# The first b block of a fused decoder layer: seven products in place of four plain quarters, with the operand slots renamed

## What is computed

```python
    z = jnp.einsum("btd,dc->btc", xn, w_in)
    u, v, b_gate, c_gate, x_in, r_a, r_b = jnp.split(z, SPLITS, axis=-1)
    ...
    y_a = jnp.einsum("btc,cd->btd", u * chunk_spatial_mix(v, w_s, b_s), w_a_out)
    ...
    y_b = jnp.einsum("btc,cd->btd", b_gate * short_conv(xp, conv_w), w_b_out)
    h = jax.nn.sigmoid(r_a) * y_a + jax.nn.sigmoid(r_b) * y_b
    out = jnp.einsum("btd,de->bte", h, w_o)
```

## Time and profile before

| What | Value |
|---|---|
| Time, median of 3 runs | 1595.23 us (1594.76 to 1595.33) |
| Time of the profiled execution | 1594.81 us |
| Its span, first to last instruction | 1593.1 us |
| TensorE matmul busy | 1583.8 us, 12361 matmuls |
| VectorE, ScalarE, GpSimd busy | 999.7, 561.7, 707.8 us |
| DMA | 187.27 MB, mean 118 GB/s |
| Granted TensorE clock | 0.999 |

### The profile page before, as it was taken

One profiled execution on the slowest core, in us unless ns is written; L12 is line 12 of the kernel. 1 busy time (PEld: TensorE's weight loads), 2 busy tenths in 40 slices (PEclk: granted clock), 3 DMA queues, 4 the chain that ended last, 5 costly groups with the idle time before them and its releaser, 6 DMA issues.

```text
span 1593.1 us, 30063 instructions
## 1 busy us (share of the span) xinstructions
PE 1583.8 (99%) x12361; PEld 1535.1 (96%) x12361; DVE 999.7 (63%) x1371; ACT 561.7 (35%) x868; POOL 707.8 (44%) x521
## 2 busy tenths in 40 slices
PE   9999999999999999999999999999999999999998
PEld 6889999999999999999978899999999999999998
DVE  7757856686683337768875574544444456685865
ACT  4223332222223335334333632222222234453544
POOL 1011444545544444535640325444444444565675
PEclk9999999999999999999999999999999999999999
DMA  6202011422413333465333402533343356673723
GB/s 220 76 1 80 28 54 34 127 76 65 126 60 129 107 107 108 153 206 181 120 114 120 146 28 74 160 107 107 107 107 107 107 147 173 214 239 107 240 106 134
DMA packets 155842, 187.27 MB, mean 118 GB/s; under 512 B 7403, under 2 KB 138083, under 8 KB 155451
## 3 DMA queue, kind: packets, MB, share of 16 engines
q1 hardware_dynamic: 152635, 182.41, 36.2%
q10 hardware_dynamic: 3072, 2.95, 0.6%
HBM read 133.74 MB, written 48.72 MB: 115 GB/s over the span
## 4 chain that ended last, share of the span: by engine, by line
PE 97%; DMA 1%; POOL 0%; SPq 0%; ACT 0%; issue 0%; DVE 0%; POOLq 0%; ACTq 0%; DVEq 0%
PE ps L439 92%; PE ps L474 2%; PE ps L551 1%; DMA tp_f<-ht_dram 1%; PE ps L534 0%; PE ps L449 0%; PE ps L733 0%; PE ps L717 0%; SPq L1032 0%; ACT tp L1709 0%; DVE tp L2508 0%; PE ps L528 0%; POOL x_late L1240 0%; DVE g L2610 0%; POOLq L178 0%
## 5 line engine op out<-in xcount | busy, mean ns | idle before, releaser
L439 PE MATMUL ps<-tp,ring_hi 128*128 128x258 f32 x7226 | 1173.5, 283 | 1.0 <-DVE g L2613 0.7
L439 PEld LDWEIGHTS ps<-tp,ring_hi 128*128 128x128 f32 x7226 | 1001.8, 190 | 2.1 <-issue 1.9
L439 PE MATMUL ps<-tp,ring_lo 128*128 128x258 f32 x3624 | 740.4, 283 | 0.0
L439 PEld LDWEIGHTS ps<-tp,ring_lo 128*128 128x128 f32 x3624 | 567.8, 190 | 0.0
L1168 POOL TENSOR_TENSOR ring_lo<-ring_f,ring_hi 128x512 fp32r<-128x512 f32 (+1 forms) x240 | 344.4, 1456 | 343.5 <-DVE ring_f L1986 209.2
L1168 POOL TENSOR_TENSOR ring_lo<-stage,ring_hi 128x512 fp32r<-128x512 f32 (+1 forms) x196 | 289.9, 1488 | 408.8 <-ACT ring_hi L1313 408.5
L1313 ACT ACTIVATE ring_hi<-ring_f 128x512 fp32r<-128x512 f32 (+1 forms) x240 | 149.9, 625 | 505.0 <-DVE ring_f L1981 166.8
L1313 ACT ACTIVATE ring_hi<-stage 128x512 fp32r<-128x512 f32 (+1 forms) x196 | 120.3, 618 | 229.6 <-PE ps L439 160.1
L1978 DVE TENSOR_TENSOR ring_f<-stage 128x512 f32<-128x512 f32 (+1 forms) x60 | 59.4, 990 | 99.0 <-DMA stage<-in_w_in 52.4
L439 PE MATMUL ps<-tp 128*128 128x512 f32 (+1 forms) x384 | 72.0, 340 | 0.0
L439 PEld LDWEIGHTS ps<-tp 128*128 128x128 f32 x384 | 59.0, 189 | 8.1
(11 more groups left out here) (271 smaller groups left out, 1447.6 us busy)
## 6 DMA issues: line engine op xcount, KB each, us to landing
stage<-in_w_in SPq DMA_DIRECT2D x24, 1024.0 KB, 5.9
ht_dram<-ht SPq DMA_DIRECT2D x44, 258.0 KB, 4.5
hid_dram<-hq SPq DMA_DIRECT2D x40, 258.0 KB, 3.0
stage<-in_w_gate SPq DMA_DIRECT2D x10, 1024.0 KB, 7.1
stage<-in_w_up SPq DMA_DIRECT2D x10, 1024.0 KB, 5.4
tp_f<-ht_dram SPq DMA_DIRECT2D x16, 516.0 KB, 6.4
stage<-in_w_down SPq DMA_DIRECT2D x8, 1024.0 KB, 5.3
tp_f<-hid_dram SPq DMA_DIRECT2D x12, 516.0 KB, 8.4
```

The costliest lines, as they stand in the source:

```text
L439: ins = pe.matmul(o, w, xc, start=first and n == 0, stop=last and n == 2, skip_group_check=onto)
```

## The change

Block 28 leaves `QORDER` and takes the seven-product form. Slot 0, free during the last three a blocks, now holds quarter 0 (p0) in place of quarter 1, which is no longer loaded. The operands of p3, p1 and p2 are loaded as block 27 finishes its products 0, 1 and 2, and those of p4, p5 and p6 as it finishes 4, 5 and 6. Splits and rests move to new places in the queues, s1 of the a blocks moves ahead of the last weight parts, and TensorE's order interleaves blocks 27, 28 and 29. `H_SLOT` and `O_SLOT` follow the renamed slots. `B_ORDER` is the order in which the b operands become ready.

```diff
-SLOT_M = [2, 0, 1, 6, 3, 4, 7, 5]
+SLOT_M = [0, 3, 1, 7, 2, 6, 4, 5]
-H_SLOT = [0, 2, 3, 1]
+H_SLOT = [3, 0, 2, 1]
+B_ORDER = [0, 3, 1, 2, 4, 5, 6]
-QORDER.update({b: (1, 3, 0, 2) for b in (B_B, B_F, B_UP0)})
+QORDER.update({b: (1, 3, 0, 2) for b in (B_F, B_UP0)})
-O_SLOT = {1: 4, 3: 7, 5: 6, 7: 5}
+O_SLOT = {1: 6, 3: 4, 5: 7, 7: 5}
 # TensorE
-            for i in range(4):
-                bank_free(B_B - 1, PLAIN_BANK[i])
-                half(B_B, i, PLAIN_BANK[i], lambda q: (b_lo, (3, 1, 4, 2)[q]))
-            for r in range(B_B + 1, B_F):
+            for r in range(B_B, B_F):
                 for p in range(7):
-                    if r == B_B + 1 and p in (1, 3, 4, 6):
-                        pe.wait_ge(b_lo, (1, 3, 4, 6).index(p) + 5)
+                    if r == B_B:
+                        pe.wait_ge(b_lo, B_ORDER.index(p) + 1)
                     product(r, p)
 # SyncE, for b in range(B_A, B_F)
                 if b == B_A + 1:
                     sp.wait_ge(prod_done, BASE[B_A + 1])
-                    ob_load(1)
+                    b_load(0)
                 if b + 2 < B_F:
                     load(b + 2)
                 if b == B_B - 1:
-                    for i, n in enumerate((3, 0, 2)):
+                    for p, i in ((3, 0), (1, 1), (2, 2)):
                         sp.wait_ge(prod_done, done(b, i))
-                        ob_load(n)
-                if b + 1 < B_F:
+                        b_load(p)
+                    gate_load_one(b + 1, 0, SPILL[0])
+                    for p, i in ((4, 1), (5, 2), (6, 3)):
+                        sp.wait_ge(prod_done, done(b, p))
+                        b_load(p)
+                        gate_load_one(b + 1, i, SPILL[i])
+                elif b + 1 < B_F:
                     gate_load(b + 1)
 # ScalarE
             for r in range(B_A + 1, B_B):
-                s1(r)
+                if r == B_A + 1:
+                    s1(r)
                 if r < B_B - 1:
                     prepare(r + 1, 0, 5)
                     if r == B_A + 1:
-                        b_split(1)
+                        b_split(0)
+                    s1(r + 1)
                     prepare(r + 1, 5)
                 else:
+                    prepare(r + 1, 0, 2)
                     b_split(3)
-                    prepare(r + 1, 0, 1)
-                    b_split(0)
-                    prepare(r + 1, 1, 2)
+                    prepare(r + 1, 2, 3)
+                    b_split(1)
+                    prepare(r + 1, 3, 5)
                     b_split(2)
-                    prepare(r + 1, 2)
+                    s1(r + 1)
+                    prepare(r + 1, 5, 6)
+                    b_split(4)
+                    prepare(r + 1, 6)
-            bt_split(0)
-            prepare(B_B + 1, 0, 2)
-            bt_split(1)
-            prepare(B_B + 1, 2, 4)
-            bt_split(2)
+            b_split(5)
+            prepare(B_B + 1, 0, 1)
+            b_split(6)
+            prepare(B_B + 1, 1, 6)
             s1(B_B + 1)
-            prepare(B_B + 1, 4, 6)
-            bt_split(3)
             prepare(B_B + 1, 6)
 # VectorE
+            def b_rest(p):
+                dve.wait_ge(b_hi, B_ORDER.index(p) + 1)
+                dve.tensor_tensor(slot(SLOTS_M[p], 1), slot_f(SLOTS_M[p], 1), slot_v(SLOTS_M[p], 0), SUB).then_inc(b_lo, 1)
 # VectorE, a blocks; last is r == 27
                 c22(r, s_turn[(r + 1) % 2][:, :], s_c[:, :])
+                if last:
+                    b_rest(3)
                 sums(r + 1, 2)
                 a_gate(r, 3, s_turn[(r + 1) % 2][:, :], c22_done)
                 c12(r, s_c[:, :])
                 if last:
                     b_rest(1)
                 sums(r + 1, 3)
                 a_gate(r, 1, s_c[:, :], c12_done)
+                dve.wait_ge(a_gated, at_r + 2)
+                c21(r, s_turn[r % 2][:, :])
                 if last:
                     b_rest(2)
-                dve.wait_ge(a_gated, at_r + 2)
-                c21(r, s_turn[r % 2][:, :])
                 a_gate(r, 2, s_turn[r % 2][:, :], c21_done)
                 if r == B_A + 1:
                     b_rest(0)
-                elif last:
-                    b_rest(3)
-            for i, n in enumerate(QORDER[B_B]):
...
-                sums(B_B + 1, i)
-                bt_rest(i)
 # VectorE, b blocks
-            for mp, r in enumerate(range(B_B + 1, B_F), 1):
+            for mp, r in enumerate(range(B_B, B_F)):
+                if mp == 0:
+                    b_rest(4)
                 sums(r + 1, 0)
...
                 b_gate(r, 0, reg(Y, both), s_turn[(r + 1) % 2][:, :], prod_done, done(r, 2))
+                if mp == 0:
+                    b_rest(5)
                 u2(r)
                 u4(r, s_c[:, :])
                 sums(r + 1, 1)
+                if mp == 0:
+                    b_rest(6)
```

More of the change, by code:

```diff
@@ L135, in h_order @@
 def h_order(mp):
-    return QORDER[B_B] if mp == 0 else (0, 3, 1, 2)
+    return 0, 3, 1, 2
 def slots_of(b):
@@ L583, in c11_read @@
                 if b < B_F:
-                    return a_gated, 4 * (b - B_B - 1 + MP - 1) + 1
+                    return a_gated, 4 * (b - B_B + MP - 1) + 1
                 if b < B_D:
@@ L922, in _, with b_load, gate_load_one @@
             bt_save(MP - 1)
[L924 to L931, removed]
+            def b_load(p):
+                if p in D_ROWS:
+                    n, src, count = D_ROWS[p], ob_dram, t_in
+                    sp.wait_ge(q_saved[n], 16 * MP)
+                else:
+                    n, src, count = D_TOTAL[p], bt_dram, total_in
+                    sp.wait_ge(ht_saved[n], 16 * MP)
+                sp.dma_start(slot_f(SLOTS_M[p], 1), src[n]).then_inc(count[n], 16)
+            def gate_load_one(b, i, n):
+                if b == B_A:
+                    sp.wait_ge(q_saved[n], 16 * 3 * MP)
+                elif b - 1 in QORDER:
+                    sp.wait_ge(pl_dve, PL_DVE[b - 1] + i + 1)
+                else:
+                    sp.wait_ge(a_gated, 4 * (b - 2 - B_A) + i + 1)
+                sp.dma_start(q[:, n], (ra_dram, rb_dram)[(b - B_A) // MP][b % MP, :, n]).then_inc(gate_in[n], 16)
             def gate_load(b, parts=None):
                 for i, n in enumerate(parts or (QORDER[b - 1] if b - 1 in QORDER else SPILL)):
[L935 to L943, removed]
+                    gate_load_one(b, i, n)
             for b in range(B_RA, B_A):
@@ L999, in _ @@
             res_load(1)
-            sp.wait_ge(a_gated, 8 * (MP - 1))
+            sp.wait_ge(a_gated, 4 * (2 * MP - 1))
             sp.dma_start(post_gain, mix_post_g[0:1, :].to_broadcast((128, D)).rearrange("p (n c) -> p n c", n=4)).then_inc(post_in, 16)
@@ L1497, in _, with b_split @@
                 gate(2, c21_done, r)
[L1499 to L1505, removed]
+            def b_split(p):
+                act.wait_ge(*((t_in[D_ROWS[p]], 16) if p in D_ROWS else (total_in[D_TOTAL[p]], 16)))
+                act.activation(slot(SLOTS_M[p], 0), slot_f(SLOTS_M[p], 1), ACT.Copy).then_inc(b_hi, 1)
             at_split(3)
@@ L1528, in h_split @@
                 act.wait_ge(h_ready, 4 * mp + i + 1)
-                act.wait_ge(prod_done, done(B_F - 1, mp - 1) if mp else done(B_B, 1))
+                act.wait_ge(prod_done, done(B_F - 1, mp - 1) if mp else done(B_B - 1, 3))
                 act.activation(h_of(n, 0, mp), g[:, 2 * mp + n // 2, n % 2], ACT.Copy).then_inc(h_hi, 1)
@@ L2338, in h_rest @@
                 dve.tensor_tensor(h_of(n, 1, mp), g[:, 2 * mp + n // 2, n % 2], h_of(n, 0, mp).bitcast(f32), SUB).then_inc(h_lo, 1)
-            for i, n in enumerate(QORDER[B_B]):
-                part, tmp = g[:, n // 2, n % 2], (s_b, s_c)[i % 2]
-                dve.wait_ge(prod_done, done(B_B, i))
-                dve.wait_ge(gate_in[n], 16 * (MP + 1))
-                if i >= 2:
-                    dve.wait_ge(h_ready, i - 1)
-                dve.tensor_tensor(tmp, reg(PLAIN_BANK[i], both), q[:, n], MUL).then_inc(pl_dve, 1)
-                dve.wait_ge(pl_dve, PL_DVE[B_B] + i + 1)
-                dve.tensor_tensor(part, part, tmp, ADD).then_inc(h_ready, 1)
-                sums(B_B + 1, i)
-                bt_rest(i)
             def b_gate(r, i, src, gated, ready, count=None):
@@ L2357, in b_gate @@
                 dve.tensor_tensor(gated, src, q[:, n], MUL).then_inc(a_gated, 1)
-                dve.wait_ge(a_gated, 4 * (MP + mp - 2) + i + 1)
+                dve.wait_ge(a_gated, 4 * (MP + mp - 1) + i + 1)
                 dve.tensor_tensor(part, part, gated, ADD).then_inc(h_ready, 1)
-            for mp, r in enumerate(range(B_B + 1, B_F), 1):
+            for mp, r in enumerate(range(B_B, B_F)):
                 last = r == B_F - 1
+                if mp == 0:
+                    b_rest(4)
                 sums(r + 1, 0)
-                dve.wait_ge(h_ready, 4 * mp)
+                if mp:
+                    dve.wait_ge(h_ready, 4 * mp)
                 if last:
```

10 lines of the change are left out of this document (removed).

## The result

The changed kernel takes 1600.58 us (median of 5 runs, 1600.36 to 1602.67) beside 1595.06 for the kernel before on the same chip: ratio 1.0037, 95% interval 1.0023 to 1.0052, 5.5 us slower. The sign and the size were forecast (1599.3 us), but one term was missing from the sum, and so was one wait. The profiled execution took 1601.03 us, its span is 1599.3 us.

The account below looks back on a forecast made before the run. TensorE, busy 99% of the span, was taken as the bound. Waits 2.2 + 1.6 + 3.65 = 7.45 less 3.4 give +4.1 us: 1594.8 + 4.1 = 1598.9, median 0.4 above, 1599.3; range 1595.3 to 1602.4 us.

Parts of the forecast that it names:

- VectorE's chain: VectorE's queue of rests, sums and gates in block 28, ahead of p1, p2 and p5: u2 done at 734.7.
- the disputed term: What GpSimd holds VectorE's operations in block 28: 6 x 1.10 + 2 x 0.37 = 7.3 us; at zero, 1593.1 us.
- Rival (a): VectorE is held less because GpSimd's parts fall into other gaps; at zero waits 1593.5 us; chance 0.26.
- The stands: TensorE in block 28 stands 2.2 us ahead of p1 and 3.65 us ahead of p5, waiting for VectorE.
- The stand ahead of p2: TensorE in block 28 runs p1 until 720.75, then stands 1.6 us until rest p2 is done at 722.35.
- the clock: Rival: the 3.65 us stand ahead of p5 lowers TensorE's clock to 1.2 GHz: 1602 to 1605 us; chance 0.06.
- the forecast 4.1: Whole kernel: TensorE's waits of 2.2 + 1.6 + 3.65 = 7.45 us, less 3.4 us gained: +4.1 us.
- the rest of p6: VectorE's rest p6 and c22 end at about 738.9, p6 due at 740.5: later waits zero.
- Edits at nothing: Renamed slots, moved s1 and the loads of p4, p5 and p6 cost nothing; cover over 5 us for each rest.
- Rival (c): A transfer decides: p5 lands more than 6 us later than worked out; from 1600 us up; chance 0.03.
- The gain of 3.4 us: Block 28: 24 fewer matmuls save 2.89 us, the plain block's holes and excess taken as 0.5; worth 3.4 us without new waits.

## Why the prediction was right, and what it lacked

**VectorE's chain: right.** The rests were forecast to end at 711.5, 717.85, 722.35, 727.3 and, with u2 behind p5's, at 734.7; the rows show 711.60, 717.83, 722.36, 727.39 and 734.73. Of the holds, 7.3 us forecast, the rows show the short ones at 1.79, 1.78, 1.79 and 1.78 against 0.70 (4 x 1.09), two rests at 3.29 and 3.40 against 2.30 (2.1), one rest at 2.79 and an addition at 1.08 with 0.5 and 0.4 more: 7.3 us. The run without the holds gave 1593.38 us where the working gave 1593.1 for holds of zero, and so the disputed term is shown. (Rival (a) names 1593.5 us for the same case; the sum gives 1593.1.)
The lock by the Trainium skill (SBUF — State Buffer, section "SBUF: two separate sides") was worked out as 1.30 for each full wait; in the changed kernel, too, they cost 1.0 to 1.1, so the rows of before were the better price.

**The stands: 2.6 and 3.5 where 2.2 and 3.65 were forecast.** For p1 TensorE was free 0.2 us sooner than the 715.6 taken, and 0.10 us pass from the rest's end (717.83) to the first matmul (717.93); for p5 it was free at 731.4, by the modelled end, and not 731.05.

**The stand ahead of p2: did not come, for a reason the forecast lacked.** Its operand was ready at 722.36, as forecast. But p1, for the most part at half clock, still kept TensorE busy then, and p2 began at 722.41, right behind the rest. The 1.6 us of the sum turned up as 1.6 us of slow p1; the run with filled stands shows the exchange, with 1.4 us ahead of p2.

**A term that was missing: the clock.** The prediction made it a rival of its own, with 0.06, in place of a term of the sum, and its argument was that the rows of before show no long stand. They show none because none was there; nothing in them spoke for a clock that stays. It also looked only at the stand ahead of p5. In fact the clock fell behind both stands. The slow p1 fell into the wait for p2 and cost nothing net; the slow p5 took 1.4 us more than at full clock. With this term the forecast 4.1 becomes 5.5, beside 5.5 (timed) and 6.2 (profiled). The rival's own price, once or twice 2.89 us, was too high: the clock was low for 3.4 us, where a product wholly at the lower level would take 24 x 0.215 = 5.2 us.
The Trainium skill (TensorE: Matmul & The Clock Gate, section "Why this matters for your kernels") says that an idle gap between bursts brings back half rate; here the trace agrees, with 0.64 and 0.67 in the stretches behind the two stands. The gaps that the page warns of are longer than the first of these stands, and the measurement decides: 2.6 us was enough here, and 2.2 us in the kernel with the order alone.

**A wait that was overlooked: the rest of p6.** The prediction let this rest and c22 be due with p6 at 740.5, and put all waits behind p5 at nothing. The rest of p6 is due before p0 of block 29, at 734.7 + 2.89 = 737.6, and by the prediction's own times it ends at 738.2: 0.6 us late. The runs at full clock show that wait (3.46 in place of 2.89 us behind p5 with the stands filled). So at full clock the forecast's sum would have been 4.7 us, and the slow p5 adds 0.9 to that, not 1.4. That the change shows no such wait is the slow p5's doing: two omissions share one place, and the total hides the smaller one.

**Edits at nothing: right, with less cover for one.** The first splits began at 707.33 and 710.34, as before. ScalarE's timeline for p5 and p6, beside the earlier trace rows:

```profile
721.69 1.94 ACT L1503 ACTIVATE tp<-tp_f 128x2064 fp32r<-128x2064 f32 x1 [0.25 <-DMA tp_f<-ob_dram]
...
726.48 1.94 ACT L1503 ACTIVATE tp<-tp_f 128x2064 fp32r<-128x2064 f32 x1 [2.34 <-DMA tp_f<-bt_dram]
```

ScalarE waited for both, so they landed just ahead of 721.7 and 726.5, where 721.3 and 725 were forecast. Their rests began at 730.7 and 736.0: over 7 us of cover each. Rival (c) was off. c22 of block 28 ended at 738.9, as forecast, and block 29 has no wait.

**The gain of 3.4 us: right.** 24 matmuls fewer are on the page, and the version whose stands are 1.2 us in all came out 2.0 us below before, where 3.4 - 1.2 = 2.2 was due. No run without any stand shows the 3.4 by itself.

## What to carry to other kernels

When an engine beside TensorE paces a stretch, add up its queue with the holds that a neighbour puts on it, from rows in which both are at work: six such holds of 1.1 us decided this change. If that sum says that TensorE will stand for more than about the longest stand in the trace you have, price a slow clock behind it as a term of the sum, and ask whether the slow product lies beside another wait, which then covers all or part of it (all for p1, 0.6 of 1.4 us for p5). When a wait stands in the program ahead of a call that does two products, count it against the first of them. And before giving up on a form with less work, look at when its operands are loaded: here the same seven products became 2 us faster than before by issuing the operands' loads and three rests earlier.

## What had not been expected of the hardware

- Behind stands of 2.6 and 3.5 us, in another kernel 2.2 and 1.8 us, and 4.3 us by itself, the granted clock was at its lower level for 3.4 us of trace time. In the kernel with the weights' load behind the operands, where a stand of 3.5 us ended at 732.66, it was so for twice as long, 2 x 0.43 x 3.6 + 2 x 0.47 x 4.0 = 6.9 us by these rows:

```profile
731.40:735.00 3.60, 2.34 (x11) 2.38 (x12) 3.57 (x5) 0.63 (x1) 1.02 (x1) 0.57 0.01 5
735.00:739.00 4.00, 4.00 (x21) 4.00 (x21) 3.96 (x5) 0.63 (x1) 2.20 (x1) 0.53 0.02 4
```

- At the lower clock a matmul of 258 columns took 0.215 us from start to start, not twice the 0.1206 of the full clock, so that 3.4 us there cost the products 1.4 to 1.6 us.
- Stands of 0.4 to 1.4 us left it at 1.00 in every trace, and one of 2.1 us did in the execution traced; the same kernel's times fell into two groups. So did those of the variant with stands of 0.8 and 0.4 us and p5's rest first, three of its four slower executions at a mean of 0.998; that the clock fell in them is not shown.
- The slow stretch does not begin at one place: with one stand by itself the clock was 0.51 from 730.9 on, 0.4 us before TensorE resumed, while in the changed kernel p5 had begun at 734.9 and the fall lay across the two stretches behind it, 0.67 and 0.77.
- An operation of VectorE that reads PSUM took 0.68 us in the midst of held ones (714.93, 729.01). Behind the second of them an addition with both inputs in SBUF took 1.08 in place of 0.70, a short hold; behind the first a rest took its unheld 2.29.
